# A two-block network on one core: high and low activations side by side in one 512-column matmul

## The reference

```python
# first block
u = rmsnorm(h, g_mix_pre);   proj = u @ w_in                     # 2048 x 10240
ya = dilated_mixture_attention(qa, ka, va) @ w_branch_a
yb = stick_breaking_attention(qb, kb, vb) @ w_branch_b
h = h + rmsnorm((sigmoid(gla) * ya + sigmoid(glb) * yb) @ w_out, g_mix_post)
up = causal_depthwise_conv(rmsnorm(h, g_ffn_pre) @ w_up, conv_w, conv_b)   # 2048 x 11264
gate_ff, value = split(up)
h = h + rmsnorm((gelu(gate_ff) * value) @ w_down, g_ffn_post)    # 5632 x 2048
h = h + sigmoid(h @ w_ple_gate) * (p @ w_ple_in)
# second block
proj = rms_norm(x, attn_norm_g) @ w_in_2 + b_in_2                # 2048 x 5888
attn = sliding_window_attention(q, k, v, sinks);  y = s5_ssm(u, ...)
ssm = y_val * sigmoid(y_gate)                                    # [y_val, y_gate] = gelu(y) @ w_glu_2 + b_glu_2
x = x + (sigmoid(g1) * (attn @ w_branch_attn_2) + sigmoid(g2) * (ssm @ w_branch_ssm_2)) @ w_out_2
val, gate = split(rms_norm(x, ffn_norm_g) @ w_up_2);  gate = causal_depthwise_conv_2(gate)
x = x + (val * gelu(gate)) @ w_down_2
return rms_norm(x, final_norm_g)
```

## Time and profile before

| | |
|---|---|
| median of 3 runs | 2889.96 us (2889.47 to 2892.05) |
| span of the profiled execution | 2887.3 us |
| mean granted TensorE clock in it | 0.986 |
| matmuls in it | 22786 |
| PE / DVE / ACT / POOL busy | 96% / 63% / 45% / 11% |
| weights moved | 492.24 MB in 512 KB pieces |

### The profile page before, as it was taken

How to read it: one execution, slowest core, us unless ns; L and a number is a source line. 1 busy time by engine, 2 the same in 40 slices (tenths; PEclk the granted TensorE clock), 3 DMA queues, 4 the chain that set the end, 5 groups by cost and what they waited for, 6 DMA issues and landing times.

```text
span 2887.3 us, 57701 instructions
## 1 busy us (share of the span) xinstructions
PE 2769.6 (96%) x22786; PEld 2750.4 (95%) x22786; DVE 1820.2 (63%) x2342; ACT 1302.8 (45%) x1514; POOL 304.8 (11%) x308
## 2 busy tenths in 40 slices
PE   7999999996999999999989989999999999999997
PEld 7999999996999999999979988899999999999997
DVE  5444545746777777764465788867566666665444
ACT  4334454344444544444344344443455445444332
POOL 1000000013000000000021676700000000000000
PEclk9999999997999999999999999999999999999999
DMA  6665555563555555566545544455656565556664
GB/s 213 182 182 174 149 150 169 168 199 93 185 174 184 187 181 184 172 203 186 176 148 155 160 139 138 137 164 180 195 167 183 178 184 183 182 176 192 187 188 132
DMA packets 137656, 496.64 MB, mean 172 GB/s; under 512 B 15280, under 2 KB 15280, under 8 KB 137392
## 3 DMA queue, kind: packets, MB, share of 16 engines
q1 hardware_dynamic: 136800, 492.24, 55.7%
q10 hardware_dynamic: 720, 2.49, 0.2%
HBM read 492.57 MB, written 2.10 MB: 171 GB/s over the span
## 4 chain that ended last, share of the span: by engine, by line
PE 83%; DVE 7%; ACT 3%; DVEq 3%; issue 2%; POOL 1%; DMA 0%; ACTq 0%; POOLq 0%; SPq 0%
PE bank L382 81%; DVE w_lo L833 2%; ACT w_hi L592 1%; DVE act_lo L864 1%; POOL hT L1382 1%; DVEq L1139 1%; PE ps_o L382 0%; DVEq L1098 0%; DVE scn L1134 0%; DVE proj L1190 0%; DVE pr L1140 0%; DVEq L1142 0%; PE ps_a L382 0%; DVEq L1118 0%; DMA par<-in_params 0%
## 5 line engine op out<-in xcount | busy, mean ns | idle before, releaser
L833 DVE TENSOR_TENSOR w_lo<-w_raw,w_hi 128x1024 fp32r<-128x1024 f32 x928 | 1135.8, 1236 | 864.6 <-ACT w_hi L592 863.8
L592 ACT ACTIVATE w_hi<-w_raw 128x1024 fp32r<-128x1024 f32 x928 | 974.6, 1053 | 1217.3 <-PE bank L382 1123.2
L382 PE MATMUL bank<-act_hi,w_hi 128*128 128x256 f32 x5600 | 1397.4, 287 | 68.2 <-DVE act_lo L864 51.1
L382 PE MATMUL bank<-act_lo,w_hi 128*128 128x256 f32 x5600 | 1385.6, 285 | 0.0
L382 PEld LDWEIGHTS bank<-act_hi,w_hi 128*128 128x128 f32 x5600 | 1082.5, 193 | 72.0 <-DVE act_lo L864 34.7
L382 PEld LDWEIGHTS bank<-act_lo,w_hi 128*128 128x128 f32 x5600 | 1083.0, 193 | 0.7
L382 PE MATMUL bank<-act_hi,w_lo 128*128 128x256 f32 x5600 | 787.4, 283 | 0.1
L382 PEld LDWEIGHTS bank<-act_hi,w_lo 128*128 128x128 f32 x5600 | 724.2, 192 | 0.3 <-DVE w_lo L833 0.3
L382 PE MATMUL bank<-f_lo,w_hi 128*128 128x256 f32 x1408 | 338.4, 280 | 0.0
L382 PE MATMUL bank<-f_hi,w_hi 128*128 128x256 f32 x1408 | 338.3, 280 | 0.0
L382 PEld LDWEIGHTS bank<-f_lo,w_hi 128*128 128x128 f32 x1408 | 264.9, 188 | 0.0
(11 more groups left out here) (200 smaller groups left out, 1649.3 us busy)
## 6 DMA issues: line engine op xcount, KB each, us to landing
w_raw<-in_w_up SPq DMA_DIRECT2D x352, 512.0 KB, 4.4
w_raw<-in_w_in SPq DMA_DIRECT2D x252, 512.0 KB, 4.3
w_raw<-in_w_down SPq DMA_DIRECT2D x176, 512.0 KB, 3.8
w_raw<-in_w_out SPq DMA_DIRECT2D x64, 512.0 KB, 4.4
w_raw<-in_w_ple_gate SPq DMA_DIRECT2D x32, 512.0 KB, 4.4
w_raw<-in_w_branch_attn SPq DMA_DIRECT2D x16, 512.0 KB, 3.5
w_raw<-in_w_branch_a SPq DMA_DIRECT2D x8, 512.0 KB, 4.2
w_raw<-in_w_branch_b SPq DMA_DIRECT2D x8, 512.0 KB, 3.5
```

Of the source, the lines that this page charges most:

```text
L382: return pe.matmul(o, l, r, start=start, stop=stop, skip_group_check=True)
L592: act.activation(w_hi[:, k, 0:n, :], w_raw[:, k, 0:n, :], ACT.Copy).then_inc(hi_ready, 1)
L833: dve.tensor_tensor(w_lo[:, k, 0:n, :], w_raw[:, k, 0:n, :], w_hi[:, k, 0:n, :].bitcast(F32), ALU.subtract).then_inc(lo_ready, 1)
```

## The change

The high and the low activations become two planes of one tensor (`act_w`, `f_w`, `y_w`, `p_w`, `x2_w`; `halves` gives the old names as views). PSUM's `bank` and `ps_a` become two halves of one tensor `ps_w[i]` of two banks. A stage can be marked `wide`. In a wide stage PE runs, per high weight tile, one matmul over both planes, 512 columns, into the bank of that output tile: columns 0 to 255 get high*high (`main_of`), 256 to 511 get low*high (`rest_of`); the eight matmuls with `w_lo` add their 256 columns to `rest`. Wide are `in`, `rest`, `out`, `up`, `down`, `ple_gate`, `out2`, `up2`, `down2`, 712 of the 928 pieces. `mix`, `in2`, `in2b`, `in2c` (beside which `ps_a` is in use), `branch`, `glu`, `branch2` and `ple` stay as they were.

The two halves are added at evacuation. For stages marked `kept`, ACT copies `rest` to SBUF (`keep_rest`), then DVE adds `main` to it (`whole_sum`), and what followed before follows on SBUF: the multiply by `rstd` (`scaled_sum`), the conv out of `up_x` (a part of `tab`), the square on ACT (one group later, `rest_and_square`), the sigmoid (`ple_open`). For `direct` stages (`out2`, `down2`) DVE adds `rest` and `main` to `hT` one after the other. `out`, `down` and `ple_gate` are now evacuated by DVE instead of ACT. In `up` and `up2` the bank is free after the sum; `conv_ready` tells ACT's gelu that the conv is done. In `ple` the sum of squares on PE moves from behind the second to behind the third piece.

```diff
@@ PE, stream
-                                    o = ps[:, c * TOK:(c + 1) * TOK]
                                     w = w_hi[:, k, t, c * P:(c + 1) * P]
-                                    mm(o, w, xh[:, x, :], j == 0 and t == 0 and c == 0, False)
-                                    mm(o, w, xl[:, x, :], False, False)
+                                    if st.wide:
+                                        mm(both[:, c, :, :], w, xw[:, :, x, :], j == 0 and t == 0, False)
+                                    else:
+                                        o = ps[:, c * TOK:(c + 1) * TOK]
+                                        mm(o, w, xw[:, 0, x, :], j == 0 and t == 0 and c == 0, False)
+                                        mm(o, w, xw[:, 1, x, :], False, False)
                             pe.wait_ge(lo_ready, q + 1)
...
-                                    last = mm(ps[:, c * TOK:(c + 1) * TOK], w_lo[:, k, t, c * P:(c + 1) * P],
-                                              xh[:, x, :], False, j == st.pieces[s] - 1 and t == n - 1)
+                                    o = both[:, c, 1, :] if st.wide else ps[:, c * TOK:(c + 1) * TOK]
+                                    last = mm(o, w_lo[:, k, t, c * P:(c + 1) * P], xw[:, 0, x, :],
+                                              False, j == st.pieces[s] - 1 and t == n - 1)
...
@@ ACT
+            def keep_rest(st, i, s, dst):
+                whole(st, i, s)
+                act.activation(dst, rest_of(st, s), ACT.Copy).then_inc(rest_kept, 1)
+            def rest_and_square(st, dst, norm):
+                def squared(n, k):
+                    act.wait_ge(evacuated["dve"], st.evac0 + n + 1)
+                    square(norm, n, k, dst[:, bass.ds(2 * n, 2), :])
+                def ep(i, s):
+                    n = i * len(st.slots) + s
+                    keep_rest(st, i, s, dst[:, bass.ds(2 * n, 2), :])
+                    if not (isinstance(n, int) and n == 0):
+                        squared(n - 1, (s - 1) % 2)
+                return ep, lambda: squared(7, 1)
...
@@ DVE
+            def whole_sum(st, i, s, dst):
+                dve.wait_ge(rest_kept, st.kept0 + i * len(st.slots) + s + 1)
+                return dve.tensor_tensor(dst, dst, main_of(st, s), ALU.add)
...
             def ffn(st, base, w, b, tiles, value_conv):
                 def ep(i, s):
-                    whole(st, i, s)
-                    ps = bank[(st.group0 + s) % 2]
-                    pair = ps[:, :].rearrange("p (c t) -> p c t", c=2)
+                    x = up_x[:, s, :, :]
+                    whole_sum(st, i, s, x).then_inc(evacuated["dve"], 1)
+                    dve.drain()
                     if s == 0 or value_conv:
-                        dve.tensor_tensor(pair, pair, over_tokens, ALU.mult)
+                        dve.tensor_tensor(x, x, over_tokens, ALU.mult)
                         dve.drain()
                     if s == 0:
-                        conv(gate_y, ps, w, b, 2 * i, tiles).then_inc(evacuated["dve"], 1)
+                        conv(gate_y, x, w, b, 2 * i, tiles).then_inc(conv_ready, 1)
...
@@ add_to_residual
-                    dve.tensor_tensor(h, h, bank[(st.group0 + s) % 2][:, :].rearrange("p (c t) -> p c t", c=2),
-                                      ALU.add).then_inc(evacuated["dve"], 1)
+                    dve.tensor_tensor(h, h, rest_of(st, s), ALU.add)
+                    dve.drain()
+                    dve.tensor_tensor(h, h, main_of(st, s), ALU.add).then_inc(evacuated["dve"], 1)
```

More of the change, by code:

```diff
@@ L100, in place @@
 def place(stages):
-    piece = group = 0
+    piece = group = kept = 0
     done = {"act": 0, "dve": 0}
@@ L105, in place @@
     for st in stages:
-        st.piece0, st.group0, st.evac0 = piece, group, done[st.evac]
+        st.piece0, st.group0, st.evac0, st.kept0 = piece, group, done[st.evac], kept
         n = st.bodies * len(st.slots)
+        kept += n if st.wide == "kept" else 0
         for _ in range(n):
@@ L278, in build @@
-        st_branch = Stage("branch", branch1, 4, (y_hi, y_lo), lambda j: (split_ready, SPLIT["y1"] + 2), "dve")
-        st_out = Stage("out", pair("w_out"), 4, act_x, main_x(SPLIT["merged"]), "act")
+                        2, act_x, None, "dve", "kept")
+        st_branch = Stage("branch", branch1, 4, y_w, lambda j: (split_ready, SPLIT["y1"] + 2), "dve")
+        st_out = Stage("out", pair("w_out"), 4, act_x, main_x(SPLIT["merged"]), "dve", "kept")
         st_up = Stage("up", [cols("w_up", 16, 0, G), cols("w_up", 16, 0, G, FF)], 22, act_x,
-                      main_x(SPLIT["ffn"]), "dve")
@@ L282, in build @@
-        st_down = Stage("down", quad("w_down", FT), 2, f_x, lambda j: (f_ready, 2 * j + 2), "act")
+                      main_x(SPLIT["ffn"]), "dve", "kept")
+        st_down = Stage("down", quad("w_down", FT), 2, f_x, lambda j: (f_ready, 2 * j + 2), "dve", "kept")
         st_ple = Stage("ple", quad("w_ple_in", 2), 2, p_x, main_x(SPLIT["ple_in"]), "act")
-        st_gate = Stage("ple_gate", pair("w_ple_gate"), 4, act_x, main_x(SPLIT["ple_gate"]), "act")
+        st_gate = Stage("ple_gate", pair("w_ple_gate"), 4, act_x, main_x(SPLIT["ple_gate"]), "dve", "kept")
@@ L567, in _ @@
             stream(st_down)
-            stream(st_ple, lambda piece: sum_squares(3) if piece == 1 else None)
+            stream(st_ple, lambda piece: sum_squares(3) if piece == 2 else None)
             stream(st_gate)
@@ L789, in ple, with ple_open @@
                     act.wait_ge(ple_used, n)
-                act.activation(sg[:, :, :], bank[(st_gate.group0 + s) % 2][:, :].rearrange("p (c t) -> p c t", c=2),
-                               ACT.Sigmoid).then_inc(evacuated["act"], 1)
+                keep_rest(st_gate, i, s, sg[:, :, :])
+            def ple_open(i, s):
+                n = i * 2 + s
+                act.wait_ge(evacuated["dve"], st_gate.evac0 + n + 1)
+                act.activation(sg[:, :, :], sg[:, :, :], ACT.Sigmoid).then_inc(sg_ready, 1)
                 if s or not isinstance(i, int) or i:
                     square(4, n - 1, (s - 1) % 2, hT[:, bass.ds(2 * n - 2, 2), :])
-            last = stream(st_gate, ple, lambda piece: round_up(3, piece) if piece < 4 else None)
-            last()
+            def ple(i, s):
+                ple_rest(i, s)
+                ple_open(i, s)
+            stream(st_gate, ple, lambda piece: round_up(3, piece) if piece < 4 else None)
+            ple_rest(3, 1)
+            ple_open(3, 1)
             act.wait_ge(halved, 1)
@@ L1267, in beside_down @@
                     discretize(n // 8 - 1)
-            last = stream(st_down, None, beside_down, last)
-            stream(st_ple, None, lambda piece: root(3) if piece == 3 else None)
+            last = stream(st_down, add_rest(st_down, m2T), beside_down, last)
+            stream(st_ple, None, lambda piece: root(3) if piece == 3 else None, last)
             def fed(c):
@@ L1278, in _ @@
             round_off(3, 0)
-            last_ple = stream(st_gate, ple, round_off_beside(3, fed))
+            stream(st_gate, ple, round_off_beside(3, fed))
+            ple_sum(3, 1)
             round_off(4, 0)
```

170 lines of the change are left out of this document (108 added, 62 removed).

## The result

| | before | changed |
|---|---|---|
| median | 2889.72 us (4 runs) | **2852.16 us** (4 runs, 2850.45 to 2853.03) |
| span of the profiled execution | 2887.3 us | 2851.1 us |
| matmuls in it | 22786 | 17090 |

The ratio is 0.9869, with a 95% interval from 0.9857 to 0.9881. The change is faster by 37.6 us; 124.8 us had been forecast, and the time lies 24 us above the upper end of the range.

What follows compares the result with a forecast made beforehand. PE, busy 96% of the span, was taken as the bound: -131.9 us from its stream and +7.1 us where stages meet give -124.8 us, from 2889.96 to 2765 us, range 2753 to 2828.

Steps and rivals of the forecast that it cites:

- The price of the 512-column matmul: Wide pieces on PE: 215 ns against the pair's 239.8 (act) or 234.4 (f), together 133.7 us saved.
- rival B: Wide matmuls: part of the surcharge is fixed and paid once, 226.5 (act) and 223.8 ns (f); 2826 us, chance 0.13.
- the half-clock term: About ten wide pieces run at half clock, where the pair already costs 2 x 213.3 ns: 1.8 us less saved.
- Rival E: Only about 2.5 ns of surcharge belongs to each matmul, the rest to the columns: 14 us saved, 2883 us, chance 0.04.
- Inside the stages: Added copy and sum fit beside PE; DVE needs 20.0 to 21.3 us per body of up, PE 21.4: cost 0.
- Rival C: DVE becomes the bound in up, 22.1 us a body instead of 21.4: 2780 to 2790 us, chance 0.14.
- Where stages meet: At stage changes the copy and the sum stand in the chain one after the other: +7.1 us in sum.
- out to up: Stage change: copy, square, sum beside it, then both POOL adds in a row before PE's sum: +1.9 us.
- rest to branch: Stage change: copy, tanh and wait for DVE's sum delay the second piece's `w_hi` about 1.4 us, partly covered: +1.0 us.
- down to ple: Stage change: same chain as out to up, and the sum of squares moves to a later piece of ple: +1.7 us.
- ple_gate to in2: Stage change: copy 0.59 and sum 0.69 us stand before the sigmoid, partly in ACT's idle time: +0.9 us.
- Rival D: fp32r streams at a fixed rate, so a 512-column matmul costs the pair's 240 ns: slower, 2897 us, chance 0.09.

Runs made afterwards that it cites:

- experiment 1: No network, only unbroken rows of 96 matmuls on the changed kernel's buffer layout: fp32r 226.7 ns at 512 columns, 120.0 at 256.
- experiment 2: Changed kernel with each 512-column matmul made two of 256 again, new evacuation kept: 2898.72 us, ratio 1.0029.
- e_pairs: The kernel of experiment 2, narrow matmul pairs with the changed kernel's evacuation: 2898.72 us, ratio 1.0029.

## Why the prediction was wrong

**What bounds the kernel: right.** PE is as full as before, its chain is still 83% of the span, and what left its stream came through: 46.5 us measured against 46.7 from the starts.

**The price of the 512-column matmul: wrong, and it is the whole miss.** The step that failed is the one from the earlier trace rows to 215 ns. The surcharge of 13.3 ns was read as a weight load that hides behind a long stream. The rows it was read from were of another operand type (plain f32, 2.5 ns on top per record of 512 columns in experiment 1) or at the other clock. At the lower clock the surcharge is absent at either length: the earlier trace rows has 213.6 ns for 256 columns, and in the changed kernel 54 distances between wide matmuls are 420 to 427 ns, where 512 columns at 1.2 GHz are 426.7. For fp32r at full clock a stream of 213 ns does not hide it: 226.7 ns in steady rows. That is rival B's 226.5 for `act`, at a chance of 0.13. B's fixed part, paid once, fits the steady rows with no offset; it does not fit those at 16 and 64 bytes, nor `f`, where B had 223.8. On top of it comes what no rival had: behind a change of width, and by the starts of the operands, it is 230.1 and 233.7 ns in the kernel. In the sum, 8 x 15.1 ns x 536 = 64.7 us and 8 x 18.7 ns x 176 = 26.3 us are missing, while the low-weight matmuls gave 8 x 0.7 ns x 536 = 3.0 us back that had not been forecast: 88.0 us. The stage changes below add 2, and the half-clock term, forecast at 1.8, came to 54 x 9.7 ns = 0.5, which takes 1.3 off: 88.7 us for the 87.2 that are missing, the rest not placed. The forecast's range had a slip in it as well: 2765 - 9.7 is 2755 and not 2753, which changes nothing here.

**The two prices before, 120 with `act` and 117.3 with `f`: misread.** B's argument took the step between them as a sign that the surcharge depends on which tile streams. In experiment 1 both buffers cost 120.0, and both stand at a difference of 0 there; in the kernel it was in the addresses (0 and 160 bytes off the weights). With `act` moved to 64 it costs 117.8 in up. In the changed kernel the same 160 bytes make `f` the dear one, 350.8 a slice, so down gained 10 ns a piece and not the 155 of the forecast.

**Rival E falls with the 13.3 ns.** The Trainium skill, page "TensorE: Matmul & The Clock Gate", section "Back-to-back issue gap", gives N / 2.4 + 2.5 ns as the gap of isolated matmuls. The bare rows of experiment 1 have it for bf16 (109.2 ns at 256 columns) and not for fp32r (120.0 at 256, 226.7 at 512). Its shape, columns plus a fixed part, fits the rows with no offset, where 13.3 in the place of 2.5 gives 226.6.

**Inside the stages: right.** DVE has two sums more per body of up and still keeps up. It waits 39.7 us for ACT in 440 / 22.3 = 19.7 bodies, 2.0 us each, so it needs 20.3 us of a body; 20.0 to 21.3 had been forecast. Rival C was not seen. As a body takes 8 x 2.79 = 22.3 us and not 21.4, the cover was not tested at the length that C spoke of.

**Where stages meet: right in mechanism and, within the noise, in size.** 7.1 us forecast, 9.1 measured in experiment 2, with an interval (1.0018 to 1.0040) of 5 to 12 us. The largest term, out to up, in the timeline of the changed kernel:

```profile
652.59 0.60 ACT L635 ACTIVATE mT<-ps_w 128x512 f32<-128x512 f32 x1 [9.10 <-PE ps_w L405]
653.08 0.62 ACT L630 ACTIVATE tab<-mT 128x512 f32<-128x512 f32 x1
653.22 0.69 DVE L968 TENSOR_TENSOR mT<-mT,ps_w 128x512 f32<-128x512 f32 x1 [8.88 <-ACT mT L635]
653.78 2.67 POOL L1437 TENSOR_TENSOR tab<-tab 128x512 f32<-128x512 f32 x2 [8.89 <-ACT tab L630]
...
656.50 1.24 PE L405 MATMUL ps_n<-tab 128*128 128x256 f32 x4 [3.95 <-POOL tab L1437]
```

Copy, square, the sum beside it, and both POOL adds in a row: the steps as forecast, and PE's wait for POOL is 3.95 us where it was 2.03, that is +1.92 for +1.9 forecast. From rest to branch a pause of 1.1 us stands where there was none, for 1.0 forecast, and at the very end it grew by 0.8. From down to ple the pauses did not grow (13.4 to 12.1 us over the whole stage change), for 1.7 forecast. From ple_gate to in2 they grew by 0.8 over both pauses there, for 0.9. In `e_pairs`, which has the same evacuation, the pauses at these two places grew by 1.0 and 2.1 us: between these two traces a single term differs by as much as it is worth.

**Rival D, the other side**, falls: wide matmuls do not cost 240. But for `f` it was close to the truth: a slice there costs what it did, within 1.2 ns.

## What to carry to other kernels

What one matmul in place of two saves must be measured for the very operand type, clock, mix of widths and starts of the operands: here it was 13.3, 6.5 or 1.7 ns a pair in steady fp32r rows, 9.7 and 0.9 with `act` and `f` in the kernel, and nothing at half clock. A bare row of 96 matmuls settles it in microseconds; run it in the mix in which the kernel will issue it. Where PE issues back to back for milliseconds, measure also how far the moving and the stationary operand stand apart modulo 256 bytes, before changing the program: a few unused bytes in the kernel before were worth more here (48 us) than the whole change (37.6).
